# The out projection's first two column chunks computed as a pair with two quads of seven products

## The chip, the cores and the metric

One core of one Trainium2 chip runs the kernel. The metric is the device time of one execution in microseconds (us). The engines are called as in the profile: PE (TensorE), DVE (VectorE), ACT (ScalarE), POOL (GpSimd), SP (SyncE).

## The reference

A decoder layer on 256 rows of 2048 features in float32, cut here to what matters:

```python
merged = sigmoid(ga) * (o_a @ w_br_fox) + sigmoid(gb) * (o_b @ w_br_dil)   # 256 x 2048
x = x + merged @ w_out                                                     # w_out 2048 x 2048
h = rms_norm(x, g_ffn)
u = h @ w_up                                                               # and then conv, silu, w_down
```

## The kernel before

**Precision and units.** Each float32 product is made of three float32r matmuls: with a = a_h + a_l and w = w_hi + w_lo, it sums a_h w_hi, a_h w_lo and a_l w_hi. Weights are taken in *units*: a tile of 256 rows (two k steps) by 512 columns, 512 KB. For unit n SP loads the tile, ACT makes the high half (`high(n)`, L1250), DVE the low half (`low(n)`, L1764), PE uses both. The halves lie in a ring of RING = 6 units: `high(n)` waits until unit n - 6 has been used. ACT and DVE walk one fixed list; at the position of unit n stand first the bank sums that wait for unit n, then `high(n + 6)` or `low(n + 6)`, then other work. PE, SP and POOL walk lists of their own.

**A plain unit** is used for both halves of the rows (r = 0, 1): 2 x 2 x 3 = 12 matmuls of 128x512.

**A quad of seven products.** For two column chunks side by side, a 2 x 2 block of weights (rows kt and kt + 4, columns of side 0 and side 1) with a 2 x 2 block of activations takes seven products in place of eight (P1 to P7, six matmuls each and quarter q). Two quarters (QU = 2) cover k steps 0 to 7. Operands on the weight side are tiles and sums of tiles, made in place in `raw_x[q]` and `raw_y[q]`. The order is P3 (raw_y as loaded), then POOL adds the tile of the other side to raw_y by an adding transfer (`third_sum`, y_summed); P1 takes raw_x as loaded; P7 takes raw_y; then DVE adds raw_x to raw_y (behind `low` of P7, y_added), P6 takes that; POOL adds a tile to raw_x (`first_sum`, waits for y_added, x_summed), P5 takes it; raw_x is loaded anew, P2 takes it, and in the gates DVE adds raw_x to raw_y once more for P4. The rest of the k steps goes in plain units (G, side, j).

**The stages around the change.** The seven gate pairs (`GATES`) use such quads already: five are for q, k and the gates of the two mixers. Then the branch projections: 4 chunks of w_fox and 4 of w_dil with 4 units each, all plain. After each chunk c of w_dil `dil_part(c)` on DVE multiplies two banks with the gate (L2103, dil_merged) and adds both branches into `tmp` (L2107, merged); one chunk later, after unit 2, PE turns tmp with eight transposes (L796, banks 4 and 5), ACT copies the high half to actA (`merged_high`, L1276, mt_hi), DVE makes the low half (`merged_low`, L1816, mt_lo). Chunk 3 is turned within the out projection.

**The out projection** then takes chunks 0, 1 and 2 in turn, 8 plain units each, with bank pairs (6, 7), (1, 3), (0, 2). Chunk 0 waits for mt_lo 6 (chunks 0 to 2 of merged are split), chunk 1 for dil_merged 4. `add_x2` adds the banks to x, which ACT's queue loads anew (2 MB, L1561) after the second unit. x2 is turned, scaled and squared chunk by chunk. Chunk 3 lies between the first products of the up projection. SP loads the out tiles with `load_late` (L560), and the first tiles of the up projection behind them.

## Time and profile before

| | |
|---|---|
| Time, median of 3 runs | 1336.95 us (1336.2 to 1337.53) |
| The profiled execution | 1336.57 us |
| Its span | 1334.6 us |
| PE busy | 1329.1 us, 100% |
| PE weight load busy | 1101.9 us, 83% |
| DVE busy | 1122.2 us, 84% |
| ACT busy | 940.6 us, 70% |
| POOL busy | 156.2 us, 12% |
| Moved by DMA | 305.73 MB, 229 GB/s |

The span is from the first to the last record of the profile; the execution's own time has 1.97 us beside it. Matmuls are pipelined: PE's busy time overlaps, so that its pace is read from the starts of matmuls.

### The profile page before, as it was taken

Reading aid. Unit: us, or ns where it says so; the run is one execution under the profiler, and the core shown is the slowest. Engines: PE = TensorE matmul, PEld = TensorE weight load, DVE = VectorE, ACT = ScalarE, POOL = GpSimd, SP = SyncE. Lnnn points to the kernel's source line nnn. Section 1 sums busy time; section 2 is a strip of 40 time slices with the busy share of each in tenths; the row PEclk is TensorE's granted clock in tenths of the full one; section 3 lists DMA queues with packets and bytes.
Section 4 is the critical chain, followed back from the end, with each engine's and each line's share of the span. In section 5 each row is a group of like instructions: output and inputs, shape, how many; then the busy total and the mean of one; then the engine's idle time right before and its main releaser. Section 6 shows DMA issues by size and latency. Waiting matters only on the chain.

```text
span 1334.6 us, 16448 instructions
## 1 busy us (share of the span) xinstructions
PE 1329.1 (100%) x6055; PEld 1101.9 (83%) x6055; DVE 1122.2 (84%) x1333; ACT 940.6 (70%) x1180; POOL 156.2 (12%) x175
## 2 busy tenths in 40 slices
PE   9999999999999999999999999999999999999999
PEld 7888888888888888888888888888888888888887
DVE  6768787888878876657789898999999999999996
ACT  6666666666666654446777778888888888888872
POOL 0121212021011000001010101111111102020200
PEclk9999999999999999999999999999999999999999
DMA  9877685758888655567879798999999999999952
GB/s 355 285 171 261 142 257 122 246 149 231 233 214 231 210 175 172 209 227 226 270 177 332 158 306 169 312 221 283 246 254 266 229 288 215 299 210 313 199 198 101
DMA packets 118175, 305.73 MB, mean 229 GB/s; under 512 B 11848, under 2 KB 13136, under 8 KB 117584
## 3 DMA queue, kind: packets, MB, share of 16 engines
q1 hardware_dynamic: 92288, 234.57, 50.4%
q0 software_dynamic: 21728, 66.07, 27.9%
q10 hardware_dynamic: 4080, 4.05, 0.9%
q8 instruction: 48, 0.79, 0.2%
q14 instruction: 31, 0.25, 0.1%
HBM read 302.55 MB, written 2.11 MB: 228 GB/s over the span
## 4 chain that ended last, share of the span: by engine, by line
PE 98%; DMA 1%; DVE 1%; ACT 0%; issue 0%; SPq 0%; ACTq 0%
PE acc L743 14%; PE acc L747 14%; PE acc L745 13%; PE acc L783 9%; PE acc L787 9%; PE acc L785 9%; PE acc L964 4%; PE acc L968 4%; PE acc L966 4%; PE acc L939 3%; PE acc L941 3%; PE acc L943 3%; PE acc L1076 1%; PE acc L768 1%; PE acc L766 1%; PE acc L764 1%
## 5 line engine op out<-in xcount | busy, mean ns | idle before, releaser
L1764 DVE TENSOR_TENSOR w_lo<-raw,w_hi 128x1024 fp32r<-128x1024 f32 x234 | 284.0, 1221 | 89.6 <-ACT w_hi L1250 88.4
L1250 ACT ACTIVATE w_hi<-raw 128x1024 fp32r<-128x1024 f32 x234 | 244.8, 1055 | 109.5 <-PE acc L747 75.9
L743 PE MATMUL acc<-w_hi,actA 128*128 128x512 f32 x664 | 261.7, 394 | 0.4 <-DVE w_lo L1764 0.3
L747 PE MATMUL acc<-w_hi,actA 128*128 128x512 f32 x664 | 259.1, 390 | 0.0
L745 PE MATMUL acc<-w_lo,actA 128*128 128x512 f32 x664 | 258.7, 390 | 0.0
L1250 ACT ACTIVATE w_hi<-raw_y 128x1024 fp32r<-128x1024 f32 x144 | 149.6, 1058 | 74.9 <-PE acc L747 22.4
L1764 DVE TENSOR_TENSOR w_lo<-raw_y,w_hi 128x1024 fp32r<-128x1024 f32 x144 | 173.2, 1220 | 23.1 <-ACT w_hi L1250 21.7
L1764 DVE TENSOR_TENSOR w_lo<-raw_x,w_hi 128x1024 fp32r<-128x1024 f32 x108 | 130.0, 1221 | 41.1 <-ACT w_hi L1250 40.9
L743 PEld LDWEIGHTS acc<-w_hi,actA 128*128 128x128 f32 x664 | 124.8, 188 | 26.3 <-issue 1.4
L747 PEld LDWEIGHTS acc<-w_hi,actA 128*128 128x128 f32 x664 | 124.7, 188 | 26.3
L745 PEld LDWEIGHTS acc<-w_lo,actA 128*128 128x128 f32 x664 | 124.8, 188 | 25.0
L1250 ACT ACTIVATE w_hi<-raw_x 128x1024 fp32r<-128x1024 f32 x108 | 111.2, 1051 | 37.8 <-DMA raw_x<-w_in 19.1
L783 PE MATMUL acc<-w_hi,actB 128*128 128x512 f32 x296 | 116.2, 393 | 0.0
L787 PE MATMUL acc<-w_hi,actB 128*128 128x512 f32 x296 | 115.4, 390 | 0.0
L785 PE MATMUL acc<-w_lo,actB 128*128 128x512 f32 x296 | 115.3, 389 | 0.0
L964 PE MATMUL acc<-w_hi,actA 128*128 128x512 f32 x224 | 88.4, 395 | 0.0
L968 PE MATMUL acc<-w_hi,actA 128*128 128x512 f32 x224 | 87.3, 390 | 0.0
L966 PE MATMUL acc<-w_lo,actA 128*128 128x512 f32 x224 | 87.2, 389 | 0.0
L2405 POOL DMA_DIRECT2D raw_y<-w_up x34 | 29.5, 867 | 458.9 <-DVE w_lo L1764 458.6
L1250 ACT ACTIVATE w_hi<-odd 128x1024 fp32r<-128x1024 f32 x63 | 66.3, 1053 | 18.5 <-PE acc L787 9.8
L1764 DVE TENSOR_TENSOR w_lo<-odd,w_hi 128x1024 fp32r<-128x1024 f32 x63 | 76.8, 1218 | 1.8 <-ACT w_hi L1250 1.8
L2178 DVE SCALAR_TENSOR_TENSOR work<-acc,smalls_sb,work 128x255 f32<-128x255 f32 (+1 forms) x176 | 72.5, 474 | 3.4 <-ACT work L1583 3.3
(296 smaller groups left out, 2598.8 us busy)
## 6 DMA issues: line engine op xcount, KB each, us to landing
raw<-w_in SPq DMA_DIRECT2D x102, 512.0 KB, 4.8
raw<-w_down SPq DMA_DIRECT2D x59, 512.0 KB, 5.7
raw_x<-w_up SPq DMA_DIRECT2D x44, 512.0 KB, 5.0
raw_y<-w_up POOLq DMA_DIRECT2D x34, 512.0 KB, 7.3
raw_x<-w_in SPq DMA_DIRECT2D x28, 512.0 KB, 4.3
raw<-w_out SPq DMA_DIRECT2D x28, 512.0 KB, 4.5
odd<-w_up SPq DMA_DIRECT2D x27, 512.0 KB, 5.2
work<-w_up SPq DMA_DIRECT2D x24, 512.0 KB, 5.4
```

The lines of the kernel that those rows point to most:

```text
L743: nc.tensor.matmul(o, lhsT=a_h, rhs=w_hi[:, s, k, :], start=first and k == 0, stop=False, skip_group_check=onto_seed)
L745: nc.tensor.matmul(o, lhsT=a_h, rhs=w_lo[:, s, k, :], start=False, stop=False, skip_group_check=onto_seed)
L747: mm = nc.tensor.matmul(o, lhsT=a_l, rhs=w_hi[:, s, k, :], start=False, stop=last and k == KU - 1, skip_group_check=onto_seed)
L783: nc.tensor.matmul(o, lhsT=a_h, rhs=w_hi[:, s, k, :], start=first and k == 0, stop=False, skip_group_check=True)
L785: nc.tensor.matmul(o, lhsT=a_h, rhs=w_lo[:, s, k, :], start=False, stop=False, skip_group_check=True)
L787: mm = nc.tensor.matmul(o, lhsT=a_l, rhs=w_hi[:, s, k, :], start=False, stop=last and k == KU - 1, skip_group_check=True)
L964: nc.tensor.matmul(o, lhsT=a_h, rhs=w_hi[:, s, k, :], start=side == 0 and j == 0 and k == 0, stop=False, skip_group_check=True)
L966: nc.tensor.matmul(o, lhsT=a_h, rhs=w_lo[:, s, k, :], start=False, stop=False, skip_group_check=True)
L968: mm = nc.tensor.matmul(o, lhsT=a_l, rhs=w_hi[:, s, k, :], start=False, stop=kt == KT - 1, skip_group_check=True)
L1250: nc.scalar.activation(w_hi[:, n % RING, :, :], src.rearrange("p (k n) -> p k n", k=KU), ACT.Copy).then_inc(hi_done, 1)
L1764: nc.vector.tensor_tensor(w_lo[:, n % RING, :, :], src.rearrange("p (k n) -> p k n", k=KU), w_hi[:, n % RING, :, :].bitcast(f32), ALU.subt ...
L2178: t = nc.vector.scalar_tensor_tensor(out=conv[:, j, lag:SEQ], in0=bank[(4, 7)[j // 2]][:, (j % 2) * SEQ:(j % 2 + 1) * SEQ - lag], scalar=s ...
```

## The change

Chunks 0 and 1 of the out projection become pair number PAIRS = 7, with two quads (k steps 0 to 7) and four plain units on each side (k steps 8 to 15). The units' order is P3, P1, P7, P6 (two quarters each), G 0 0, P5, G 0 1, G 1 0, P2, G 0 2, P4, G 0 3, G 1 1, G 1 2, G 1 3, and then the eight units of chunk 2 (C). The names G00, G01, G10 below are plain units by side and j.

- Activations: `merged_high` for merged chunks 0 and 1 copies each bank twice, once to `odd` in float32; after chunk 1 `make_merged` forms four sums, each from the last; four `merged_part_high` on ACT and four `merged_part_low` on DVE split them, and ACT copies -P1 (two copies).
- P3 waits for the four parts (h_part_lo 8) in place of mt_lo 6, P1 for dil_merged 4.
- P1's sum is copied by ACT from bank 0 to bank 1 and P6's from bank 0 to bank 3; the next product in bank 0 and the plain units wait for the copies (g_p1, g_v).
- P4's operand is summed by an adding transfer of POOL to raw_y behind the low half of P6 (y_summed), where the gates have an addition on DVE.
- The load of x is issued after P3's second quarter.
- Counts of the semaphores that the up projection shares with the pair (y_added, x_summed and so on) go up accordingly, and the first raw_x and raw_y tiles of the up projection are loaded behind P2 and P4 of the pair.

The diff, cut to its core:

```diff
 BR_UNIT = GATE_UNIT + len(GATES)
 OUT_UNIT = BR_UNIT + 4 * UPR
-FF_UNIT = OUT_UNIT + 3 * UPR
+
+
+def out_units():
+
+    def product(name):
+        return [("H", PAIRS, name, q) for q in range(QU)]
+
+    def plain(side, *js):
+        return [("G", PAIRS, side, j) for j in js]
+
+    units = product("P3") + product("P1") + product("P7") + product("P6") + plain(0, 0)
+    units += product("P5") + plain(0, 1) + plain(1, 0) + product("P2") + plain(0, 2)
+    units += product("P4") + plain(0, 3) + plain(1, 1, 2, 3)
+    return units + [("C", u) for u in range(UPR)]
+
+
...
+OUTS = out_units()
+OUT_LOADS = [unit for unit in OUTS if unit[0] != "H"]
+OUT_LOAD_AT = {unit: k for k, unit in enumerate(OUT_LOADS)}
+OUT_AT = {unit: OUT_UNIT + n for n, unit in enumerate(OUTS)}
+FF_UNIT = OUT_UNIT + len(OUTS)
...
                     load_gate_b22(c + 1, q)
             for m in range(RAW_SLOTS, 4 * UPR):
                 load_late(BR_UNIT + m, br_tile(m))
...
+
+            def load_out(k):
+                unit = OUT_LOADS[k]
+                if unit[0] == "G":
+                    _, c, side, j = unit
+                    src = pair_tile(side, c, 2 * QU + j)
+                else:
+                    src = pair_tile(2, PAIRS, unit[1])
+                s = raw_use(OUT_AT[unit])[0]
+                sp.dma_start(raw[:, s, :].rearrange("p (k n) -> p k n", k=KU), src).then_inc(w_loaded[s], 16)
+
+            for k in range(RAW_SLOTS):
+                sp.wait_ge(lo_done, OUT_UNIT - RAW_SLOTS + k)
+                load_out(k)
+            for n, unit in enumerate(OUTS, OUT_UNIT):
+                if unit[0] != "H":
+                    k = OUT_LOAD_AT[unit] + RAW_SLOTS
+                    if k < len(OUT_LOADS):
+                        sp.wait_ge(lo_done, n)
+                        load_out(k)
+                    continue
+                _, c, name, q = unit
+                if name == "P5":
+                    sp.wait_ge(lo_done, n)
+                    load_gate_b21(c, q)
+                elif name == "P2":
+                    sp.wait_ge(lo_done, n)
+                    load_b11(0, q)
+                elif name == "P4":
+                    sp.wait_ge(lo_done, n)
+                    load_b22(0, q)
             sp.wait_ge(o_lo, NHEADS)
             for k in range(2):
                 load_unit(LOADS[k])
...
+            def out_product(n, name, q):
+
+                if q == 0:
+                    if name == "P3":
+                        pe.wait_ge(o_lo, NHEADS)
+                        pe.wait_ge(h_part_lo, 8)
+                    elif name == "P1":
+                        pe.wait_ge(dil_merged, 4)
+                        pe.wait_ge(h_part_hi, 12)
+                    elif name == "P7":
+                        pe.wait_ge(g_c22, PAIRS)
+                    elif name == "P6":
+                        pe.wait_ge(g_p1, PAIRS + 1)
+                    elif name == "P5":
+                        pe.wait_ge(g_v, PAIRS + 1)
+                o = bank[OUT_BANKS[name]]
+                pe.wait_ge(lo_done, n)
...
+            def out_plain(n, side, j):
+
+                pe.wait_ge(mt_lo, 6 if j < 2 else 8)
+                pe.wait_ge(lo_done, n)
+                s = n % RING
+                for r, o in enumerate((bank[6], bank[0]) if side else (bank[1], bank[3])):
+                    if r and j == 0:
+                        pe.wait_ge(g_u0 if side else g_v, PAIRS + 1)
...
+            for n, unit in enumerate(OUTS, OUT_UNIT):
+                if unit[0] == "H":
+                    out_product(n, unit[2], unit[3])
+                    if unit == ("H", PAIRS, "P1", QU - 1):
                         pe.wait_ge(merged, 4)
                         transpose_block(lambda r, col: tmp[:, r, col:col + P], bank[4:6], mt_ready)
-                    elif u == 2:
-                        turn_x2(c - 1)
+                elif unit[0] == "G":
+                    out_plain(n, unit[2], unit[3])
...
+                    if unit == ("G", PAIRS, 1, PLAIN - 1):
+                        turn_x2(0)
+                else:
+                    u = unit[1]
+                    if u == 0:
+                        pe.wait_ge(g_c22, PAIRS + 1)
+                    rows_unit(n, actA, (KU * u, KU * u + 1), (bank[2], bank[0]), u == 0, u == UPR - 1)
+                    if u == 2:
+                        turn_x2(1)
 
             def turn_up(rows, ready):
 
...
                     kt = 4 * c + 2 * b
+                    if c < 2:
+                        nc.scalar.activation(merged_turned(c)[:, 2 * b:2 * b + 2, :],
+                                             bank[4 + b][:, :].rearrange("p (j s) -> p j s", j=2), ACT.Copy)
                     nc.scalar.activation(actA[:, kt:kt + 2, 0:SEQ],
                                          bank[4 + b][:, :].rearrange("p (j s) -> p j s", j=2),
                                          ACT.Copy).then_inc(mt_hi, 1)
+
+            def merged_part_high(name, made):
+                act.wait_ge(h_made, made)
+                nc.scalar.activation(merged_part(name)[:, :, 0:P], merged_sum[name], ACT.Copy).then_inc(h_part_hi, 1)
 
             def x2_squares(c):
...
-            for c in range(3):
-                for u in range(UPR):
-                    high(OUT_UNIT + UPR * c + u + RING)
-                    if u == 1 and c == 0:
-                        act.wait_ge(merged, 4)
-                        act.dma_start(xr[:, :, :], x_rows).then_inc(x_again, 16)
-                    if u == 2 and c == 0:
-                        merged_high(3)
-                    elif u == 2:
-                        x2t_copy(c - 1, bank[4:6])
-                    elif u == 4 and c == 2:
-                        part_high("P3")
-                        part_high("P1")
-                    elif u == 5 and c == 2:
-                        part_high("P7")
-                        part_high("P6")
-                x2_squares(c)
+                    elif c == 3 and u == 0:
+                        merged_part_high("P5", 9)
+                        merged_part_high("P7", 10)
+                        merged_part_high("P6", 11)
+                        merged_part_high("P3", 12)
+                    elif c == 3 and u == 1:
+                        act.wait_ge(mt_lo, 2)
+                        for half in range(2):
+                            nc.scalar.activation(own[:, 0, :, half * P:half * P + P],
+                                                 gate_quarter(0, 0, half).bitcast(f32), ACT.Copy, scale=-1.0)\
+                                .then_inc(h_part_hi, 1)
+
+            def out_sum(n, name):
+
+                act.wait_ge(used, n + 1)
+                if name == "P1":
+                    act.wait_ge(dil_merged, 3)
+                    nc.scalar.activation(bank[1], bank[0], ACT.Copy, scale=-1.0).then_inc(g_p1, 1)
+                else:
+                    nc.scalar.activation(bank[3], bank[0], ACT.Copy, scale=-1.0).then_inc(g_v, 1)
+
+            for n, unit in enumerate(OUTS, OUT_UNIT):
+                if unit in (("H", PAIRS, "P1", QU - 1), ("H", PAIRS, "P6", QU - 1)):
+                    out_sum(n, unit[2])
+                high(n + RING)
+                if unit == ("H", PAIRS, "P3", QU - 1):
+                    act.wait_ge(merged, 4)
+                    act.dma_start(xr[:, :, :], x_rows).then_inc(x_again, 16)
+                elif unit == ("H", PAIRS, "P1", QU - 1):
+                    merged_high(3)
+                elif unit == ("G", PAIRS, 1, 2):
+                    x2_squares(0)
+                elif unit == ("G", PAIRS, 1, PLAIN - 1):
+                    x2t_copy(0, bank[4:6])
+                elif unit == ("C", 1):
+                    x2_squares(1)
...
+            def make_merged():
+
+                x11, x21, x12, x22 = (merged_sum[name] for name in ("P6", "P7", "P3", "P5"))
+                nc.vector.tensor_tensor(x22, x21, x22, ALU.subtract).then_inc(h_made, 1)
+                dve.wait_ge(h_made, 9)
+                nc.vector.tensor_tensor(x21, x11, x21, ALU.subtract).then_inc(h_made, 1)
+                dve.wait_ge(h_made, 10)
+                nc.vector.tensor_tensor(x11, x11, x22, ALU.subtract).then_inc(h_made, 1)
+                dve.wait_ge(h_made, 11)
+                nc.vector.tensor_tensor(x12, x12, x11, ALU.subtract).then_inc(h_made, 1)
+
+            def merged_part_low(name, n_hi):
+                dve.wait_ge(h_part_hi, n_hi)
+                to = merged_part(name)
+                nc.vector.tensor_tensor(to[:, :, P:2 * P], merged_sum[name], to[:, :, 0:P].bitcast(f32), ALU.subtract)\
+                    .then_inc(h_part_lo, 1)
+
             for c in range(4):
                 for u in range(4):
                     if u == 3:
                         if c:
                             merged_low(c - 1)
                             dve.wait_ge(mt_ready, 2 * c)
+                        if c == 2:
+                            make_merged()
                         dil_part(c)
                     low(BR_UNIT + 16 + 4 * c + u + RING)
                     if c == 0 and u == 0:
                         out_low(15)
+                    elif c == 3 and u == 1:
+                        merged_part_low("P5", 7)
+                        merged_part_low("P7", 8)
+                        merged_part_low("P6", 9)
+                        merged_part_low("P3", 10)
 
             def add_x2(n, c, banks):
                 dve.wait_ge(used, n + 1)
...
+            def out_rows(r, side):
+                return xr[:, r, side * NB:side * NB + NB]
+
+            def add_bank(b, rows):
+                return nc.vector.tensor_tensor(rows, bank[b], rows, ALU.add)
+
+            def out_bank_sums(n, unit):
+
+                if unit == ("H", PAIRS, "P5", QU - 1):
+                    dve.wait_ge(x_again, 16)
+                    dve.wait_ge(used, n + 1)
+                    add_bank(0, out_rows(0, 1)).then_inc(g_u0, 1)
+                elif unit == ("G", PAIRS, 0, 1):
+                    nc.vector.tensor_tensor(out_rows(1, 1), out_rows(1, 1), bank[7], ALU.subtract).then_inc(g_u1, 1)
+                elif unit == ("G", PAIRS, 1, 0):
+                    add_bank(7, out_rows(1, 0)).then_inc(g_v7, 1)
+                elif unit == ("G", PAIRS, 0, PLAIN - 1):
+                    dve.wait_ge(used, n + 1)
+                    add_bank(1, out_rows(0, 0))
+                    dve.wait_ge(g_v7, PAIRS + 1)
+                    add_bank(3, out_rows(1, 0)).then_inc(x2_done, 1)
+                elif unit == ("G", PAIRS, 1, PLAIN - 1):
+                    dve.wait_ge(used, n + 1)
+                    dve.wait_ge(g_u1, PAIRS + 1)
+                    add_bank(0, out_rows(1, 1)).then_inc(g_c22, 1)
+                    dve.wait_ge(g_u0, PAIRS + 1)
+                    add_bank(6, out_rows(0, 1)).then_inc(x2_done, 1)
+                elif unit == ("C", UPR - 1):
+                    add_x2(n, 2, (bank[2], bank[0]))
+
+            for n, unit in enumerate(OUTS, OUT_UNIT):
+                out_bank_sums(n, unit)
+                low(n + RING)
+                if unit == ("H", PAIRS, "P7", 0):
+                    merged_low(3)
+                elif unit == ("C", 3):
+                    make_sums()
+                elif unit == ("C", 5):
+                    part_low("P3")
+                    part_low("P1")
+                elif unit == ("C", 6):
+                    part_low("P7")
+                    part_low("P6")
 
             def x2_norm():
 
...
                 prepare_dil(12 + c).then_inc(prep_ready, 1)
+            third_sum(PAIRS, 0)
+            third_sum(PAIRS, 1)
+            first_sum(PAIRS, 0)
+            first_sum(PAIRS, 1)
+            for q in range(QU):
+                pool.wait_ge(lo_done, OUT_AT["H", PAIRS, "P6", q])
+                nc.gpsimd.dma_start(raw_y[:, q, :].rearrange("p (k n) -> p k n", k=KU),
+                                    w_out_v[:, KU * (QU + q):KU * (QU + q) + KU, 0:NB], accum_op=ALU.add)\
+                    .then_inc(y_summed[q], 16)
 
             def add_tile(side, i, kt_pair, to, done):
```

## Rows read from the trace of the kernel before

**Rows 1.** Page: the chain that ended last, shares by engine.
```profile
PE 98%; DMA 1%; DVE 1%; ACT 0%; issue 0%; SPq 0%; ACTq 0%
```

**Rows 2.** Windows (stretch, length, PE, PEld, DVE, ACT, POOL busy, clock, DMA share, GB/s).
```profile
293.20:334.00 40.80, 40.80 (x184) 33.85 (x182) 32.29 (x29) 26.69 (x32) 4.83 (x4) 1.00 0.75 205
...
553.60:598.90 45.30, 45.27 (x208) 37.66 (x209) 24.37 (x23) 20.73 (x26) 0.00 (x0) 1.00 0.65 229
```

**Rows 3.** Timeline of PE, 549.5 to 555.5 (start, length, what).
```profile
549.76 1.03 PE L796 MATMUL acc<-smalls_sb,tmp 128*128 128x128 f32 x8
550.55 0.48 PE L743 MATMUL acc<-w_hi,actB 128*128 128x512 f32 x1
...
552.69 0.39 PE L743 MATMUL acc<-w_hi,actB 128*128 128x512 f32 x1
...
553.14 0.39 PE L747 MATMUL acc<-w_hi,actB 128*128 128x512 f32 x1
553.63 0.47 PE L743 MATMUL acc<-w_hi,actA 128*128 128x512 f32 x1
```

**Rows 4.** Timeline of PE, 0 to 14: the nine warm-up matmuls.
```profile
1.32 4.21 PE L864 MATMUL acc<-actB 128*128 128x512 f32 x9 [1.32 <-POOL actB L2354]
```

**Rows 5.** Timeline of DVE before the out projection, chunk 2 of the branch.
```profile
539.30 1.23 DVE L1764 TENSOR_TENSOR w_lo<-raw,w_hi 128x1024 fp32r<-128x1024 f32 x1 [1.50 <-ACT w_hi L1250]
540.45 1.28 DVE L1816 TENSOR_TENSOR actA<-acc,actA 128x512 fp32r<-128x512 f32 x2
541.86 1.29 DVE L2103 TENSOR_TENSOR work<-acc,work 128x512 f32<-128x512 f32 x2
...
544.33 1.22 DVE L1764 TENSOR_TENSOR w_lo<-raw,w_hi 128x1024 fp32r<-128x1024 f32 x1
...
553.63 1.29 DVE L2103 TENSOR_TENSOR work<-acc,work 128x512 f32<-128x512 f32 x2
```

**Rows 6.** Timeline of DVE, 613 to 621: sums and parts of x2.
```profile
613.40 0.68 DVE L1892 TENSOR_TENSOR odd<-work 128x512 f32<-128x512 f32 x1
614.12 0.69 DVE L1894 TENSOR_TENSOR odd<-work,odd 128x512 f32<-128x512 f32 x1
...
620.05 0.68 DVE L1832 SCALAR_TENSOR_TENSOR actB<-work,actB 128x512 fp32r<-128x512 f32 x1
620.65 1.22 DVE L1764 TENSOR_TENSOR w_lo<-raw_x,w_hi 128x1024 fp32r<-128x1024 f32 x1
```

**Rows 7.** Timeline of DVE, gate pair: P7's low half and its addition.
```profile
340.50 1.23 DVE L1764 TENSOR_TENSOR w_lo<-raw_y,w_hi 128x1024 fp32r<-128x1024 f32 x1 [0.20 <-ACT w_hi L1250]
341.76 1.23 DVE L1773 TENSOR_TENSOR raw_y<-raw_y,raw_x 128x1024 f32<-128x1024 f32 x1
342.90 2.44 DVE L1764 TENSOR_TENSOR w_lo<-raw_y,w_hi 128x1024 fp32r<-128x1024 f32 x2
```

**Rows 8.** Timeline of ACT, branch stage: two halves of a turned chunk.
```profile
539.18 1.06 ACT L1276 ACTIVATE actA<-acc 128x512 fp32r<-128x512 f32 x2
```

**Rows 9.** Timeline of ACT, gate pair: two high halves in succession.
```profile
339.40 2.01 ACT L1250 ACTIVATE w_hi<-raw_y 128x1024 fp32r<-128x1024 f32 x2 [2.40 <-DMA raw_y<-w_in]
```

**Rows 10.** DMA: issue of x; adding transfers (L2366); issues 558 to 563.
```profile
559.48 0.39 ACTq L1561 DMA_DIRECT2D work<-x  x1
...
DMA to landing us min/median/max: 5.8/6.2/9.5
...
work<-x ACTq DMA_DIRECT2D x1, 2048.0 KB, 10.7
raw<-w_out SPq DMA_DIRECT2D x1, 512.0 KB, 10.7
...
raw<-w_out SPq DMA_DIRECT2D x1, 512.0 KB, 9.7
```

**Rows 11.** Groups of ACT by line and form: copy from bank to bank.
```profile
L1616 ACT ACTIVATE acc<-acc 128x512 f32<-128x512 f32 x11 | 6.6, 602 | 0.0
```

132 lines of the change are left out of this document (74 added, 58 removed).

## The prediction

> **What bounds the kernel now.** I read the page first: a span of 1334.6 us and a chain of work that is 98% PE [rows 1]. Then the windows: in the stretch of the first two chunks of the out projection, and in a whole pair of gate columns, PE is busy practically all the time at a granted clock of 1.00 [rows 2]. Then PE's timeline: two matmuls start 0.45 us apart with one between them, so one starts every 0.227 us; a unit of twelve takes 2.72 us, eight transposes 0.79 us. The only hole near the change is the start of the out projection: the last branch matmul starts at 553.14, the first one of the out projection at 553.63 instead of 553.37 (it waits for the low part of the third merged chunk, mt_lo 6): 0.26 us [rows 3]. So the span is the number of matmuls plus PE's waits. A matmul saved is worth 0.227 us, and every wait put before PE costs its whole length. DVE and ACT are read for one question only: are they in time when PE asks? All times below are on the clock of the profile of before, with P3 able to start at 553.37.
>
> **Removed from PE.** Two plain chunks are 16 units x 12 = 192 matmuls. The pair is 14 product units x 6 + 8 plain units x 12 = 180. Saved: 12 x 0.227 = 2.72 us. The 0.26 us hole goes too, since P3 no longer waits for mt_lo 6. Gain: 2.98 us. The two sets of transposes stay.
>
> **Added to DVE before the pair.** This is the term to work through, since DVE runs its list in order. Columns: what it does, when it starts.
> At 539.30 the low half of P3 first quarter is made [rows 5]. ACT now makes four copies of a turned chunk instead of two; two took 1.06 [rows 8], so the last comes at about 541.3, and DVE's second merged_low of this chunk starts at 541.35 and takes 0.6. Then make_merged: four 128x512 subtractions, each waiting for the last; a dependent one starts 0.72 after its forerunner, an independent one 0.60 [rows 6], so 3 x 0.72 + 0.6 = 2.8: 541.95 to 544.75. Before, DVE began dil_part(2) at 541.86; now 544.75. It takes 2.47 (541.86 to 544.33, where the next low half starts [rows 5]): to 547.2. Three low halves (P3 second, P1 both) start 1.14 apart [rows 7]: to 550.65 (ACT has the high halves ready: that of P1's first quarter at 544.6, four merged_part_high at the pace of such copies, two in 1.06 [rows 8], to 547.75, the next high half to 548.85). Four merged_part_low at 0.6: to 553.05. **P3 asks at 553.37: hidden, with 0.3 us to spare.** Next the low half of P7 first quarter with the addition behind it; a low half, its addition and the step to the next instruction take 2.40 [rows 7]: 555.5, and this is y_added for quarter 0. Then merged_low(2), two at 0.6: 556.7. Only now dil_part(3), which DVE did at 553.63 before [rows 5]: two products of 1.29 together: **dil_merged reaches 4 at 558.05**. None of this waits for anything; DVE is simply full from 541.3 on.
>
> **P1's wait.** P1 starts bank 0, which the last branch chunk fills, so it waits for dil_merged 4. PE asks after P3's twelve matmuls, at 556.1. New wait 558.15 - 556.1 = 2.05 us. Queued behind on PE is everything. P1 then runs to 560.85, the transposes to 561.65 (merged 4 comes at 559.3), P7 to 564.4.
>
> **P6's wait.** On DVE follow the sum tmp (to 559.2), P7's second low half and its addition: y_added of quarter 1 at 561.65. On ACT the high half of P6's second quarter waits for that addition; behind it in ACT's list stand the issue of the x load, the high half of the first plain unit and only then the copy of P1's sum from bank 0 to bank 1, which P6 waits for. 561.7 + 2 x 0.96 (high halves start 0.96 apart [rows 9]) + 0.4 for the issue of the x load [rows 10] and 0.1 for the steps between = 564.2, + 0.60 for a bank to bank copy [rows 11] = 564.8. PE asks at 564.4: 0.5 us with the restart.
>
> **The wait that decides.** Row 1 of the first plain unit waits for g_v, the copy of P6's sum to bank 3. In ACT's list that copy stands behind the high halves of P5's second quarter, G01 and G10. P5's high half needs raw_x of that quarter after the adding transfer, which POOL can issue only at y_added = 561.7. From issue to landing such a transfer took 5.8 to 9.5 us, median 6.2 [rows 10]. But here 2 MB of x are asked for at about 562.7, 1 us behind it. A plain tile issued 0.4 us before the x load in the profile took 10.7 us, as long as the x load itself, and the next one, issued 2.3 us behind x, 9.7 us [rows 10]. A transfer under x is the nearest row, so I take 10: landing 571.7. Then three high halves, 3 x 0.96, and the copy, 0.6, with the steps between 0.1: g_v at 575.3. PE would be there (P6 564.9 to 567.7, row 0 to 569.0) at 569.0: **6.3 us**. Bounds: with 5.8 the landing is 567.5, g_v 571.1, the wait 2.1; with 13 (x's 10.7 lengthened by the two adding transfers for P4 and the tiles that are now under way with it) the wait is 9.3.
>
> The Trainium skill, DMA: Bandwidth & Descriptors, "Issuing engines are not separate DMA queues", says that transfers of all issuing engines run on the same 16 DMA engines and interleave; the rows above agree (10.7 us beside x), and if they did not interleave, the sum would go by the 5.8 bound.
>
> **Behind it.** The second quarter's P2 load waits in SP's queue for P5's low half (about 574), landing 578.5; high halves and low halves to 582, then the bank sum g_u0 at 582.7, which the row 1 of G10 asks for at 583.7: hidden by 1 us. The P4 operand by transfer is asked for at 563 and 564 and used after 580: hidden, also from its own price; against the gate pair it spares DVE two additions of 1.22, which lie beside PE and buy nothing here. At chunk 2 PE waits for g_c22: DVE starts 0.27 after the last matmul and takes 0.65, the transposes of x2 cover 0.79: 0.2 us. What ACT, SP and POOL have more of in the branch stage is covered: PE's units there last 2.72 with 1.06 of ACT, and DMA is at 0.65 in the stretch of the change [rows 2]. The copy of -P1 to its own tile ends at 550. From chunk 2 on nothing changes but the place of x2_squares(1), on ACT, beside 2.72 us units.
>
> **Sum.** -2.98 + 2.05 + 0.5 + 6.3 + 0.2 = +6.1 us. The profiled execution took 1336.57 (span 1334.6 and 1.97 around it), the median of the three runs is 1336.95: 1342.7 on the first, **1343.0** on the median. 0.2% is 2.7 us, about what this kernel's measurement can tell from no change.
>
> **Rivals.**
> *A, faster: the cover holds.* In the gate pair the same products run with the same rings without a hole in PE: 40.8 us of 40.80 busy [rows 2]. If DVE reaches dil_part(3) by 554.7 instead of 556.7, P1 does not wait, y_added of quarter 1 comes at 559.6, the adding transfer, issued 3 us ahead of x, lands in 5.8 at 565.4, and g_v is there at 569.0. Then nothing waits but chunk 2's start: -2.98 + 0.2 = -2.8, 1334.2. For it: the gates' pairs, with the same pace of loads and halves. Against: there no chunk is merged, turned and split on DVE in the six units ahead, and no x is loaded. 2 us less on DVE's list of 15.4 us (541.3 to 556.7) is the point from which it decides.
> *B, no change: the backlog comes, but the adding transfer lands early (5.8).* The wait on g_v is 2.1: +1.9, 1338.9. If DVE is 1 us faster besides, it is near 0.
> *C, slower still: the clock falls.* The nine warm-up matmuls, which ran after idleness, took 4.21 us [rows 4] where nine at 0.227 take 2.04. If a wait of 6.3 us on g_v leaves PE at the 1.2 GHz level for as long, another 2.2 us: +8.3, 1345.2. PE's waits near the change are 0.26 us and none [rows 2, 3], so this profile is silent on what a long one does. The Trainium skill, TensorE: Matmul & The Clock Gate, Part 1, says that the clock is halved after an idle stretch and comes back with sustained work; the warm-up row agrees, and by that rule this rival and not the main case would come.
> *D: the change doesn't do what it says.* All products and loads are in the list PE walks; twelve fewer matmuls are certain. Not given a chance.
>
> **Chances.** The DVE sum rests on a list without gaps, each duration from a row; the landing under x is the loose term. Main case 0.43, C 0.25, B 0.16, A 0.16. Slower by over 0.2% is main and C with a little of B: 0.70; within 0.2%: 0.15; faster: 0.15. Range: the low bound of B less 1 us of DVE error, about 1337, to C with the long landing, 1336.95 + 9.1 + 2.2 = 1348: 1337 to 1348. The main case alone: 1339.5 to 1346.
>
> **What the new profile would show.** DVE's timeline without a gap from the second merged_low of the chunk to dil_part(3), whose products start near 556.7 instead of 553.6 after a P3 at 553.4; an idle of PE before P1 released by DVE's gb products, of about 2 us; one of 2 to 9 us in the first plain unit's second row, released by ACT's copy of bank 0 to bank 3, with ACT itself waiting for DMA raw_x before three high halves; the x load under way at the same time. Right on the gain: 12 matmuls fewer. The granted clock in the stretch behind that wait tells C. Wrong if ACT does not wait for raw_x, if DVE shows idle time between 545 and 556, or if PE's wait before P1 is absent.

## The result: 1346.57 us, 9.9 us slower, with the wait where it was forecast and the slow clock behind it

The changed kernel takes 1346.57 us (median of six runs, 1346.28 to 1348.75), the kernel before beside it 1336.72 (six runs, 1336.2 to 1337.53): a ratio of 1.0077, 95% interval 1.0066 to 1.0088. Forecast were 1343.0 and a range of 1337 to 1348. The profiled execution took 1347.68 with a span of 1345.7.

The page of the kernel after: the span, the DMA queues (packets, MB, share of 16 engines), and the chain that ended last.

```profile
span 1345.7 us, 16482 instructions
...
q1 hardware_dynamic: 91744, 233.53, 49.9%
q0 software_dynamic: 23360, 69.21, 29.0%
...
PE 95%; DVE 2%; DMA 2%; ACT 1%; issue 1%; SPq 0%; ACTq 0%; DVEq 0%
```

PE's share of the chain fell from 98% [rows 1] to 95%. What PE waited for, by line and releaser (us in total, times, the longest):

```profile
PE acc L1162 <- ACT acc L1700: 8.5, 1, 8.5
PE acc L1142 <- DVE work L2257: 1.6, 1, 1.6
PE acc L931 <- POOL actB L2558: 1.3, 1, 1.3
PE acc L810 <- issue: 0.6, 1, 0.6
```

The first two are new and lie in the changed stage: row 1 of G00 waits for ACT's copy of P6's sum, and P1 waits for DVE's products of the last branch chunk. The third is in the unchanged start, and the fourth, at 457.41, lies ahead of the change too. PE's timeline of the kernel after puts a place to each:

```profile
550.65 1.03 PE L863 MATMUL acc<-smalls_sb,tmp 128*128 128x128 f32 x8
...
554.26 0.39 PE L1142 MATMUL acc<-w_hi,actB 128*128 128x512 f32 x1
...
556.75 0.39 PE L1146 MATMUL acc<-w_hi,actB 128*128 128x512 f32 x1
558.73 0.50 PE L1142 MATMUL acc<-w_hi,own_parts 128*128 128x512 f32 x1 [1.59 <-DVE work L2257]
...
565.04 0.39 PE L1146 MATMUL acc<-w_hi,own_parts 128*128 128x512 f32 x1
565.27 0.39 PE L1142 MATMUL acc<-w_hi,actB 128*128 128x512 f32 x1
...
569.12 0.39 PE L1166 MATMUL acc<-w_hi,actA 128*128 128x512 f32 x1
...
578.04 0.79 PE L1162 MATMUL acc<-w_hi,actA 128*128 128x512 f32 x1 [8.53 <-ACT acc L1700]
578.63 0.63 PE L1164 MATMUL acc<-w_lo,actA 128*128 128x512 f32 x1
579.06 0.63 PE L1166 MATMUL acc<-w_hi,actA 128*128 128x512 f32 x1
...
582.90 0.45 PE L1146 MATMUL acc<-w_hi,actB 128*128 128x512 f32 x1
583.18 0.39 PE L1142 MATMUL acc<-w_hi,actB 128*128 128x512 f32 x1
```

How to read it against the forecast. The branch's last transposes start at 550.65, where they started at 549.76 before [rows 3]: 0.89 us came in ahead of the change and belong to this execution (in the profiles of runs 2 and 7 below, with the same code up to there, they start at 549.86 and 549.87), so every time of the prediction is to be read 0.9 later here. P3 follows the last branch matmul at the usual step: no hole. P1 would start at 556.98 and starts at 558.73: 1.75. P6 starts at 565.27 without a wait. Row 1 of G00 would start at 569.35 and starts at 578.04: 8.69. Behind it matmuls start 0.43 apart, and from 583.18 on 0.23 apart again.

Windows of the kernel after (stretch, length, busy time of PE, PEld, DVE, ACT, POOL, granted clock, DMA share, GB/s):

```profile
557.00:569.00 12.00, 10.41 (x50) 8.55 (x50) 9.98 (x10) 5.14 (x7) 4.81 (x4) 1.00 0.71 195
569.00:578.00 9.00, 0.51 (x3) 0.09 (x1) 2.35 (x4) 3.43 (x4) 0.00 (x0) 0.71 1.07 259
578.00:583.00 5.00, 4.96 (x12) 3.89 (x13) 3.56 (x4) 1.28 (x2) 0.00 (x0) 0.50 1.09 306
583.00:590.00 7.00, 7.00 (x32) 5.77 (x31) 6.05 (x7) 3.91 (x4) 0.00 (x0) 1.00 0.89 313
```

The granted clock is 0.50, the 1.2 GHz level, for the 5 us behind the long wait. The DMA share is 1.07 and 1.09 while PE waits and behind it; in the stretch of the change it was 0.65 before [rows 2].

DVE's timeline of the kernel after shows the full list that was forecast:

```profile
541.34 1.50 DVE L1970 TENSOR_TENSOR actA<-acc,actA 128x512 fp32r<-128x512 f32 x2
542.75 0.68 DVE L2281 TENSOR_TENSOR odd<-odd 128x512 f32<-128x512 f32 x1
...
545.53 1.28 DVE L2257 TENSOR_TENSOR work<-acc,work 128x512 f32<-128x512 f32 x2
...
557.40 1.28 DVE L2257 TENSOR_TENSOR work<-acc,work 128x512 f32<-128x512 f32 x2
...
561.10 1.22 DVE L1927 TENSOR_TENSOR raw_y<-raw_y,raw_x 128x1024 f32<-128x1024 f32 x1
```

And ACT's, with the wait for the adding transfer ahead of three high halves (L1369) and the copy (L1700):

```profile
562.37 0.39 ACTq L1708 DMA_DIRECT2D work<-x  x1
...
574.56 1.06 ACT L1369 ACTIVATE w_hi<-raw_x 128x1024 fp32r<-128x1024 f32 x1 [7.76 <-DMA raw_x<-w_out]
575.52 1.99 ACT L1369 ACTIVATE w_hi<-raw 128x1024 fp32r<-128x1024 f32 x2
577.41 0.57 ACT L1700 ACTIVATE acc<-acc 128x512 f32<-128x512 f32 x1
```

DMA issues of the kernel after from 562 to 575 (KB each, median us to landing):

```profile
work<-x ACTq DMA_DIRECT2D x1, 2048.0 KB, 9.7
raw_y<-w_out POOLq DMA_DIRECT2D x2, 512.0 KB, 15.7
raw_x<-w_out POOLq DMA_DIRECT2D x1, 512.0 KB, 11.9
```

The third row is P5's adding transfer of the second quarter, issued 0.3 us behind x; the second row is P4's two.

**The books.** From the branch's last transposes to the first matmul of the up projection PE needed 72.03 us before (549.76 to 621.79) and 82.17 after (550.65 to 632.82): +10.14. That is -2.72 (twelve matmuls) - 0.26 (the hole) + 1.75 (P1) + 8.69 (g_v) + 2.42 (twelve matmuls took from 578.04 to 583.18, 5.14, for 2.72) + 0.15 (chunk 2, which starts at 609.99, 0.94 after its transposes, for 0.79) = +10.03; the missing 0.1 is of the size of what the first matmuls behind a wait take longer (P1's twelve took 2.90, not 2.72). This length, below called the stage, is free of what varies ahead of it, and is given for every experiment. Each stage is read from one profiled execution, so that small differences in it are not to be leaned on.

### The profile page after: what moved, and what is told of

It is laid out like the page before. It is cut to its first block, busy times and chain, and to the rows that moved or that the text cites. A ratio compares the mean times of both kernels' runs of the same rounds, so it can differ in the third digit from the quotient of the medians.

```text
span 1345.7 us, 16482 instructions
## 1 busy us (share of the span) xinstructions
PE 1330.0 (99%) x6043; PEld 1100.7 (82%) x6043; DVE 1137.9 (85%) x1352; ACT 952.0 (71%) x1198; POOL 163.7 (12%) x181
## 3 DMA queue, kind: packets, MB, share of 16 engines
q1 hardware_dynamic: 91744, 233.53, 49.9%
q0 software_dynamic: 23360, 69.21, 29.0%
## 4 chain that ended last, share of the span: by engine, by line
PE 95%; DVE 2%; DMA 2%; ACT 1%; issue 1%; SPq 0%; ACTq 0%; DVEq 0%
PE acc L810 12%; PE acc L814 12%; PE acc L812 12%; PE acc L850 9%; PE acc L854 9%; PE acc L852 9%; PE acc L1031 4%; PE acc L1035 4%; PE acc L1033 4%; PE acc L1010 3%; PE acc L1008 3%; PE acc L1006 3%; PE acc L1193 1%; PE acc L831 1%; PE acc L835 1%; PE acc L833 1%
## 5 line engine op out<-in xcount | busy, mean ns | idle before, releaser
L1918 DVE TENSOR_TENSOR w_lo<-raw,w_hi 128x1024 fp32r<-128x1024 f32 x226 | 273.7, 1219 | 73.5 <-ACT w_hi L1369 72.4
L1369 ACT ACTIVATE w_hi<-raw 128x1024 fp32r<-128x1024 f32 x226 | 236.0, 1054 | 86.0 <-PE acc L814 44.8
L810 PE MATMUL acc<-w_hi,actA 128*128 128x512 f32 x600 | 236.4, 394 | 0.0
L814 PE MATMUL acc<-w_hi,actA 128*128 128x512 f32 x600 | 233.9, 390 | 0.0
L812 PE MATMUL acc<-w_lo,actA 128*128 128x512 f32 x600 | 233.5, 389 | 0.0
L1369 ACT ACTIVATE w_hi<-raw_y 128x1024 fp32r<-128x1024 f32 x152 | 158.2, 1058 | 84.1 <-PE acc L814 23.1
L1918 DVE TENSOR_TENSOR w_lo<-raw_y,w_hi 128x1024 fp32r<-128x1024 f32 x152 | 182.8, 1219 | 25.0 <-ACT w_hi L1369 23.6
L1918 DVE TENSOR_TENSOR w_lo<-raw_x,w_hi 128x1024 fp32r<-128x1024 f32 x114 | 137.2, 1220 | 50.9 <-ACT w_hi L1369 50.6
L1369 ACT ACTIVATE w_hi<-raw_x 128x1024 fp32r<-128x1024 f32 x114 | 117.5, 1051 | 52.2 <-DMA raw_x<-w_in 21.3
L814 PEld LDWEIGHTS acc<-w_hi,actA 128*128 128x128 f32 x600 | 112.6, 188 | 23.9
L810 PEld LDWEIGHTS acc<-w_hi,actA 128*128 128x128 f32 x600 | 112.7, 188 | 23.2 <-issue 0.6
L812 PEld LDWEIGHTS acc<-w_lo,actA 128*128 128x128 f32 x600 | 112.8, 188 | 22.6
L1031 PE MATMUL acc<-w_hi,actA 128*128 128x512 f32 x224 | 88.5, 395 | 0.0
L1035 PE MATMUL acc<-w_hi,actA 128*128 128x512 f32 x224 | 87.3, 390 | 0.0
L1033 PE MATMUL acc<-w_lo,actA 128*128 128x512 f32 x224 | 87.2, 389 | 0.0
L1369 ACT ACTIVATE w_hi<-odd 128x1024 fp32r<-128x1024 f32 x63 | 66.3, 1053 | 20.1 <-PE acc L854 9.8
```

The source lines that it names most:

```text
L810: nc.tensor.matmul(o, lhsT=a_h, rhs=w_hi[:, s, k, :], start=first and k == 0, stop=False, skip_group_check=onto_seed)
L812: nc.tensor.matmul(o, lhsT=a_h, rhs=w_lo[:, s, k, :], start=False, stop=False, skip_group_check=onto_seed)
L814: mm = nc.tensor.matmul(o, lhsT=a_l, rhs=w_hi[:, s, k, :], start=False, stop=last and k == KU - 1, skip_group_check=onto_seed)
L1031: nc.tensor.matmul(o, lhsT=a_h, rhs=w_hi[:, s, k, :], start=side == 0 and j == 0 and k == 0, stop=False, skip_group_check=True)
L1033: nc.tensor.matmul(o, lhsT=a_h, rhs=w_lo[:, s, k, :], start=False, stop=False, skip_group_check=True)
L1035: mm = nc.tensor.matmul(o, lhsT=a_l, rhs=w_hi[:, s, k, :], start=False, stop=kt == KT - 1, skip_group_check=True)
```

## The experiments

The theory: two lists in fixed order (DVE's before P1, ACT's before g_v) and one late landing make the waits, and the half clock adds 2.4. Rivals: the adding transfers are slow by themselves; the waits stand one behind the other, so that removing one uncovers the next.

**1. x asked for later**

```diff
-                if unit == ("H", PAIRS, "P3", QU - 1):
+                elif unit == ("H", PAIRS, "P6", QU - 1):
                     act.wait_ge(merged, 4)
                     act.dma_start(xr[:, :, :], x_rows).then_inc(x_again, 16)
```

> One edit to the changed kernel: ACT issues the 2 MB load of x behind the bank copy and the high half at the position of P6's second quarter, not behind P3's second quarter. In the changed kernel the adding transfer to raw_x (second quarter) took 11.9 us with x beside it; the other three took 6.0 to 6.2. Theory (x beside it is what makes it late): it lands about 6.2 us after its issue near 562.6, so near 569; the copy g_v comes near 572.5, the wait of PE on it shrinks from 8.7 us to about 3, the granted clock stays at 1.00 or falls only briefly, and x lands near 584, before or within 2 us of the bank sum that needs it. Time about 1338 to 1341. Rival (the adding transfers for P4 queued right behind it, or the SP tiles, are what slow it): the landing stays above 9 us, the wait above 6 us, the time above 1344.

1350.4 us, ratio 1.0102 (1.0087 to 1.0117), stage 85.03. PE's timeline:

```profile
572.07 0.50 PE L1162 MATMUL acc<-w_hi,actA 128*128 128x512 f32 x1 [2.73 <-ACT acc L1700]
...
589.46 0.80 PE L1162 MATMUL acc<-w_hi,actA 128*128 128x512 f32 x1 [7.29 <-DVE work L2324]
```

DMA issues of this run from 555 to 575:

```profile
raw_x<-w_out POOLq DMA_DIRECT2D x2, 512.0 KB, 6.0
raw_y<-w_out POOLq DMA_DIRECT2D x2, 512.0 KB, 10.3
```

The landing was as the theory has it: P5's adding transfer of the second quarter took 6.1 us (11.9 with x beside), and the wait on g_v fell from 8.5 to 2.7. So the adding transfers are not slow by themselves; P4's two are still right behind it here. But x, issued at 576.76, was now what the bank sum g_u0 lacked, and row 1 of G10 waited 7.3 us. The clock fell behind the wait of 2.7 too. The time is a miss (1338 to 1341 expected): I had not followed x to the instruction that reads it.

**2. The copy ahead of the three high halves**

```diff
-                high(n + RING)
+                if unit == ("H", PAIRS, "P6", QU - 1):
+                    for late in (3, 2, 1):
+                        high(n - late + RING)
+                if unit not in (("H", PAIRS, "P7", 0), ("H", PAIRS, "P7", 1), ("H", PAIRS, "P6", 0)):
+                    high(n + RING)
```

> One edit to the changed kernel: in ACT's list the copy of P6's sum to bank 3 (g_v) stands ahead of the high halves of P5 second quarter, G01 and G10, which follow it in their order; nothing else moves. Theory (the copy itself had all it needed at 568 and only stood behind ACT's wait for raw_x): the wait before the second row of G00 goes; PE then runs G00 and P5's first quarter and waits for the low half of P5's second quarter, which comes 2.4 us after the landing near 574.5, so about 5 us instead of 8.7. Time 1341 to 1344. Rival (the copy waits for something else, such as a bank or PE): the wait stays at 8 to 9 us and the time at 1346 to 1347.

1346.62 us, 1.0073 (1.0058 to 1.0088), stage 82.03. The wait on g_v is gone, and PE's timeline has two others:

```profile
575.90 0.80 PE L1142 MATMUL acc<-w_hi,actB 128*128 128x512 f32 x1 [4.49 <-DVE w_lo L1922]
...
585.96 0.50 PE L1162 MATMUL acc<-w_hi,actA 128*128 128x512 f32 x1 [2.19 <-DVE work L2328]
```

The first is P5's second quarter, which needs the same late transfer itself; the second is the bank sum. The place in ACT's list was a cause of the wait on g_v and not of the loss. The wait before P5 was forecast at about 5, the one on the bank sum was not, and the time of 1341 to 1344 was a miss.

**3. The last chunk's products earlier in DVE's list**

```diff
-                        if c:
+                        if 0 < c < 3:
                             merged_low(c - 1)
...
+                    if c == 3 and u == 3:
+                        dve.wait_ge(mt_ready, 6)
+                        merged_low(2)
```

> One edit to the changed kernel: DVE makes the low halves of merged chunk 2 (merged_low(2)) behind dil_part(3) and the low half and addition of P7's second quarter, not ahead of dil_part(3); PE waits for them before the next transposes. Theory (P1 waits for DVE's full list, and y_added of the second quarter comes at the end of that list): the two copies of 0.6 us leave the list ahead of both, so P1's wait shrinks from 1.75 to about 0.55 us, while the transfer is issued 1.2 us earlier and x not earlier than the same addition. The wait on g_v changes by at most 1.2 us. Time 1344 to 1346. Rival (P1 waits for PE's own last branch unit or for ACT): the wait before P1 stays at 1.7 us.

1345.75 us, 1.0066 (1.0051 to 1.0081), stage 80.74. P1's wait went from 1.6 to 0.4 and the one on g_v from 8.5 to 5.8; the transposes behind P1 now waited 1.9 for the merged_low that was moved. As expected (1344 to 1346): the wait before P1 is DVE's list. In the whole time the gain is within the spread (1344.24 to 1346.87).

**4. Matmuls in place of the wait**

```diff
+                    if r and j == 0 and not side:
+                        for _ in range(34):
+                            nc.tensor.matmul(bank[2][:, :], lhsT=own_parts[:, 0:P], rhs=own_parts[:, 0:NB],
+                                             start=True, stop=True)
```

> One edit to the changed kernel: 34 more matmuls of 128x512 into a bank that nothing uses yet, between the two rows of G00, ahead of the wait on g_v; their results are overwritten, and the output stays the reference's. They fill 34 x 0.227 = 7.7 us of the wait of 8.7 us. Theory (the half clock behind the wait is a cost of its own, 12 matmuls at 0.43 in place of 0.227): the wait shrinks to 1 us, g_v does not move, the clock stays at 1.00 and the time falls by about 2.4 us to 1344. Rival (the clock behind the wait is not the wait's doing, or PE was held back there by something else): the matmuls behind g_v still start 0.43 us apart and the time stays at 1346.5 or rises.

1347.68 us (1345.75 to 1347.76), 1.0081 (1.0064 to 1.0098), stage 81.10 in the profiled run. Windows of the same stretches as above:

```profile
569.00:578.00 9.00, 7.76 (x34) 6.12 (x34) 2.71 (x4) 3.44 (x4) 0.00 (x0) 1.00 1.07 261
578.00:583.00 5.00, 5.00 (x23) 4.13 (x22) 3.21 (x3) 1.46 (x2) 0.00 (x0) 1.00 1.08 329
```

The clock stays at 1.00 and 23 matmuls fit where 12 did, so the idleness is what let it fall. The stage is only 1.07 shorter, not 2.4: row 1 started 0.37 later in it (the landing took 12.3 us), and G10's row 1 then waited 0.6 for the bank sum, which it had not waited for while the clock was slow. In the whole time no gain can be seen, and the forecast of 1344 was a miss.

**5. DVE's new sums and parts on GpSimd**

```diff
-                nc.vector.tensor_tensor(x22, x21, x22, ALU.subtract).then_inc(h_made, 1)
+                nc.gpsimd.tensor_tensor(x22, x21, x22, ALU.subtract).then_inc(h_made, 1)
...
-                nc.vector.tensor_tensor(to[:, :, P:2 * P], merged_sum[name], to[:, :, 0:P].bitcast(f32), ALU.subtract)\
+                nc.gpsimd.tensor_tensor(to[:, :, P:2 * P], merged_sum[name], to[:, :, 0:P].bitcast(f32), ALU.subtract)\
```

> One edit to the changed kernel: POOL, not DVE, makes the four sums of make_merged and the four low halves of the parts (POOL stands idle there). Theory (DVE's full list makes P1 wait and y_added of the second quarter late): DVE's list before dil_part(3) is 5.2 us shorter, dil_part(3) starts as soon as PE's last branch unit is done, the wait before P1 goes to 0, and y_added of quarter 1 comes at about 560 instead of 562.3 (PE's last branch unit, two products, the sum, a low half and its addition still stand before it). With x issued right behind, the transfer still takes 10 to 12 us: the wait on g_v stays at 7 to 9 us, since PE arrives 1.75 us earlier as well. Time 1344 to 1346. Rival (the late transfer is only the backlog's doing): the wait on g_v falls under 5 us and the time under 1342.

1352.0 us, 1.0112 (1.0095 to 1.0129), stage 85.95. Timelines of POOL and of DVE:

```profile
547.86 2.17 POOL L2589 TENSOR_TENSOR odd<-odd 128x512 f32<-128x512 f32 x1
...
556.48 1.73 POOL L2598 TENSOR_TENSOR own_parts<-odd,own_parts 128x512 fp32r<-128x512 f32 x1
557.74 2.90 POOL L2598 TENSOR_TENSOR actB<-odd,actB 128x512 fp32r<-128x512 f32 x2
```

```profile
548.80 2.32 DVE L1918 TENSOR_TENSOR w_lo<-raw_y,w_hi 128x1024 fp32r<-128x1024 f32 x1
...
556.13 5.59 DVE L1918 TENSOR_TENSOR w_lo<-raw_x,w_hi 128x1024 fp32r<-128x1024 f32 x1 [2.79 <-ACT w_hi L1369]
```

A miss. Low halves that take 1.22 alone took 2.32 and 5.59. The first ends 1.1 after POOL's subtraction beside it (550.03), the second 1.1 after POOL's last (560.64): they did not share, DVE's instruction stood until POOL's were done. The Trainium skill, SBUF — State Buffer, "SBUF: two separate sides", says that of a VectorE instruction with two SBUF inputs and a GpSimd instruction that reads SBUF the one that starts first holds their common port for its whole length, and the other is blocked. These rows agree with the blocking; in the second case POOL's subtractions that started later, from 556.48 on, went ahead of DVE's of 556.13 all the same. P3 waited 2.8, P1 2.9, and row 1 of G00 5.7 on g_v.

**6. x in two halves, the first behind P7's first quarter, the second behind G01** (an issue moved and split; VectorE waits for the second half at chunk 2)

> One edit to the changed kernel: x is loaded in two halves by columns, the first (chunks 0 and 1, 1 MB) behind the high half that waits for the late adding transfer, the second behind G01. Theory (x beside the transfer costs 5.7 us, and moving all of x behind it only moved the wait to the bank sum, 7.3 us in e1): the transfer lands in 6.2 us, the wait on g_v is 2.7 us as in e1, the first half of x lands in about 6 us, near 576, and the bank sum waits at most 1 us; P1's 1.7 us stays. Half clock behind g_v costs up to 2 us. Time 1338 to 1341. Rival (what made it late is the number of transfers, whatever their size): over 1344.

1346.05 us, 1.0072 (1.0056 to 1.0087), stage 81.30: 2.6 on g_v, then 3.9 on the bank sum, since P2's plain loads landed late (ACT waited 8.8 us for one, to 580.13). The adding transfer took 5.9 with nothing of x beside it, but the half of x issued behind it took 12.0. A miss (1338 to 1341 expected): half as much x in this stretch is not enough less.

**7. 2, 5 and the split together**

> Three edits to the changed kernel together: the sums and low halves on POOL (as e5), x in two halves behind the late transfer (as e6, the first half issued right behind P5 second quarter's high half), and the copy g_v ahead of those three high halves (as e2). Theory (the waits found are all that stands between the 12 saved matmuls and the time): no wait of PE over 0.3 us in the pair, clock at 1.00; time = before - 2.7 - 0.26 + 0.2, that is about 2.8 us below before, 1334. Rival (the pair's own demand on DMA, or contention that no edit here touches, is a further cost): another wait of over 1 us appears and the time stays above that of before.

1351.47 us, 1.0111 (1.0096 to 1.0126), stage 86.50. No wait on g_v, but 2.8 before P3 and 1.3 before P1 (the blocking of run 5), and 8.5 on the bank sum. A miss (1334 expected): the waits found so far were not all that stood between the saved matmuls and the time.

**8. P4's operand by VectorE**

```diff
-            for q in range(QU):
-                pool.wait_ge(lo_done, OUT_AT["H", PAIRS, "P6", q])
-                nc.gpsimd.dma_start(raw_y[:, q, :].rearrange("p (k n) -> p k n", k=KU),
-                                    w_out_v[:, KU * (QU + q):KU * (QU + q) + KU, 0:NB], accum_op=ALU.add)\
-                    .then_inc(y_summed[q], 16)
```

> One edit to the changed kernel: P4's operand is summed by DVE behind P2's low half, as in the gate pairs, and the two adding transfers behind P6 are left out. Theory (they are issued behind the late transfer of raw_x and land long before P4): the wait on g_v shrinks by at most 1 us, since less is under way beside x and the transfer; DVE's two additions of 1.22 us delay the low half of G02 and the bank sum g_u0 behind it by up to 2.4 us, which adds a wait of 0 to 2 us before G10's second row. Time 1345 to 1348, no clear change. Rival (the two transfers, each worth more than one plain load, are what doubles the landing time): the landing falls to 8 us, the wait on g_v to 5, the time to 1343.

1346.74 us, 1.0078 (1.0063 to 1.0093), as expected the time of the changed kernel; stage 80.97. The wait on g_v is 8.0, and P5's transfer still took 11.4 us. In runs 2, 3 and 4 and in the changed kernel, where P4's two transfers are behind it, it took 11.2 to 12.3; in runs 1, 6, 7 and 9, with P4's two but no x beside it, 5.9 to 6.2. So x nearly doubles the landing, and P4's two add nothing that can be told. The profiled stage is 1.2 shorter, 0.5 of it on g_v and most of the rest behind it, where the slow clock lasted 3.2 us and not 4.9; the medians show no such gain. In the whole time P4's operand by transfer neither gains nor costs here, and the two additions that it spares DVE are hidden too.

**9. The half of x that the pair reads, issued in the branch stage** (at 535.98 instead of 562.37; the other half behind G03)

```diff
+                    if c == 2 and u == 1:
+                        act.wait_ge(merged, 2)
+                        act.dma_start(xr[:, :, 0:2 * NB], x_rows[:, :, 0:2 * NB]).then_inc(x_again, 16)
```

> One edit to the changed kernel: x for chunks 0 and 1 (1 MB) is loaded in the branch stage, as soon as the gate columns under it are used up (merged 2), where DMA is half idle, and the rest of x at G03. Nothing of x is under way from 555 to 590. Theory (2 MB of x in the stretch where the pair's transfers are most dense is the loss; e1 and e6 only moved it onto the P2 loads and the bank sum): the adding transfer lands in 6.2 us, the wait on g_v is 2.7 us, the P2 loads land in 6 to 8 us, no wait on g_u0; P1's 1.7 us stays; half clock behind g_v costs 1.5 to 2.4 us. Time 1336.7 - 3.0 + 1.7 + 2.7 + 2.0 + 0.2 = 1340.3, 1339 to 1342. Rival (the pair's own transfers fill DMA by themselves): a wait of over 2 us is left on P5, P2 or G10, time over 1343.

1342.68 us (1340.19 to 1345.08), 1.0044 (1.003 to 1.0058), stage 78.70: 3.9 us less than the changed kernel. The wait on g_v is 2.8; 1.6 stay before P1, 1.6 on the bank sum, and 1.3 are new before chunk 2. Windows:

```profile
554.00:562.00 8.00, 6.41 (x33) 5.05 (x32) 7.89 (x10) 2.07 (x3) 1.20 (x1) 1.00 0.48 77
562.00:570.00 8.00, 7.05 (x32) 5.49 (x30) 5.15 (x5) 5.99 (x8) 3.66 (x3) 1.00 0.79 138
570.00:580.00 10.00, 8.13 (x30) 6.61 (x31) 5.39 (x6) 3.73 (x5) 0.00 (x0) 0.83 1.07 312
```

Without x, DMA is full from 570 on all the same, from the pair's own transfers and the tiles that SP lets go when low halves are done. The time lies between the two forecasts (1339 to 1342, and over 1343 if the pair's own transfers fill DMA).

**10. 9 with both lists reordered** (DVE: last chunk's products one low half and its addition earlier; ACT: both copies of sums ahead of the high halves that they stood behind)

> e9 and three moves in the lists: DVE does dil_part(3) ahead of P7 first quarter's low half and addition; ACT copies P1's sum ahead of P6 second quarter's high half; ACT copies P6's sum (g_v) ahead of the high halves of P5 second quarter, G01 and G10. Nothing is left out or put on another engine. Theory (list order is the rest of the loss): no wait before P1, none on g_v, up to 1 us before P5's second quarter (its transfer is issued at 562.3, lands at 568.5, its low half is ready at 571, PE asks at 570), clock at 1.00. Time 1336.7 - 3.0 + 0.2 + 0 to 1 = 1334 to 1335. Rival (a cost of the pair that no edit here touches): the time stays at or above that of before although PE shows no wait over 1 us.

1344.93 us, 1.0059 (1.0046 to 1.0072), stage 79.21. P1's wait is gone, g_v's 1.3, but the bank sum's 4.8: P2's load landed at 577.5, after ACT had waited 5.5 us for it. Two things are in this. PE was at the bank sum's place 3.5 us earlier than in run 9. And the edit itself made the load late: with the last chunk's products ahead of P7's first addition, POOL could issue P5's first transfer only at 560.25 (556.53 in run 9), and SP the load of P2 behind it only at 568.74 (566.70).

```profile
560.25 1.20 POOL L2583 DMA_DIRECT2D raw_x<-w_out  x1 [9.89 <-DVE raw_y L1936]
```

So the bank sum ran at 582.19, 0.3 earlier than in run 9, for a PE that was there 3.5 earlier. A miss by 10 us.

**11. 10 with P4's operand by VectorE**

> e10 with P4's operand summed by DVE as in the gate pairs, and without the two adding transfers behind P6. Theory (once nothing is late, P4's operand has more than 10 us by either way): the same time as e10 within 0.5 us. If the transfer for P4 is worth something, DVE's two additions of 1.22 us delay the low halves of P2 second quarter and G02 and the bank sum g_u0: up to 1.5 us slower. If instead the adding transfers cost DMA time that the P2 loads lack, it is faster by up to 1 us.

1342.78 us (1342.14 to 1343.23), 1.0044 (1.0031 to 1.0058), stage 76.86: 2.15 us less than run 10. The windows of run 10 and then of run 11:

```profile
570.00:580.00 10.00, 7.67 (x33) 5.74 (x31) 6.01 (x7) 4.19 (x6) 0.00 (x0) 1.00 1.07 318
```

```profile
570.00:580.00 10.00, 7.09 (x31) 5.26 (x29) 9.93 (x10) 6.36 (x7) 0.00 (x0) 1.00 0.76 257
```

P2's loads were there at 572.55 and 575.14 and the bank sum's wait went from 4.8 to 3.2, now from DVE's list with the two additions back in it. The executions of the two runs do not overlap (run 10 from 1343.83 up), and the gain is more than either forecast had (the same within 0.5, or up to 1 faster). With x out of this stretch and DMA full, the two adding transfers cost more than the additions that they spare.

**12. 11 with the bank sum one place earlier**

```diff
-                if unit == ("H", PAIRS, "P5", QU - 1):
+                if unit == ("G", PAIRS, 0, 0):
                     dve.wait_ge(x_again, 16)
-                    dve.wait_ge(used, n + 1)
+                    dve.wait_ge(used, OUT_AT["H", PAIRS, "P5", QU - 1] + 1)
```

> Edit: the kernel of e11 (half of x loaded in the branch stage, the two lists of VectorE and ScalarE reordered, the fourth product's operand by VectorE), and VectorE's sum of the half used bank (g_u0), which row 1 of unit G10 waits for, stands one low half earlier in VectorE's list, ahead of the low half of P2's second quarter instead of behind it, its addition and the low half of G02. List theory: in e11 P5's last matmul was done by about 575.5 and the sum started at 580.23; it now starts near 576.6 and G10's second row near 577.6 instead of 580.97; the wait of 3.2 us goes to 0.3, and PE's half clock behind it (about 2 us) goes too if a shorter wait doesn't bring it; the low half of P2's second quarter comes at 578.5, still before PE asks for it. So 3 us less than e11's 1342.8 if the clock falls all the same, 5 less if it doesn't: 1338 to 1340, and even so not below the kernel before, since a wait of 1 us on g_v, the steps of 0.6 and 0.7 and the later start of the out projection are left. Rival (the matter is DMA): the next late thing is a low half whose tile has not landed, the wait moves to P2's first product, and the time stays within 1 us of e11's.

1342.36 us (1338.45 to 1342.98), 1.0036 (1.0023 to 1.0048), stage 76.63. Expected were 1338 to 1340, a miss. The wait of 3.2 is gone and the low half of P2 came in time. PE's timeline has another in its place, and DVE's shows why:

```profile
602.28 0.78 PE L811 MATMUL acc<-w_hi,actA 128*128 128x512 f32 x1 [2.87 <-DVE work L2334]
602.86 0.63 PE L813 MATMUL acc<-w_lo,actA 128*128 128x512 f32 x1
```

```profile
600.40 1.23 DVE L1925 TENSOR_TENSOR w_lo<-raw,w_hi 128x1024 fp32r<-128x1024 f32 x1 [1.26 <-ACT w_hi L1368]
601.54 1.28 DVE L2334 TENSOR_TENSOR work<-acc,work 128x512 f32<-128x512 f32 x2
```

Chunk 2 waits for the last bank sums (g_c22). PE's last matmul of the pair started at 598.14, but the sums stand in DVE's list behind a low half whose tile landed only at 599.3, so they started at 601.54, and the clock fell behind that wait too. The gain of 0.4 on run 11 is within the spread: the rival's pattern, a landing that is late elsewhere, though not at P2, where I had put it.

## Why the prediction was right

**The direction and the place: right.** The kernel became slower, 9.9 us where 6.1 were forecast. Named were three waits and their releasers, and the two longer ones came; the long one is released by the copy of line 1700, with ACT waiting for raw_x ahead of it, x under way beside. Run 1 (no x beside, landing 6.1) and run 2 (copy first, no wait there) show both of its parts.

**The gain: right.** -2.72 and -0.26, read off directly.

**P1's wait, 2.05: measured 1.75.** The list on DVE was forecast to reach the last products at 556.7; less 0.9 it did at 556.5. Run 3 shows it is the list. Rival A (DVE quick enough, 1334.2) fell with that: 0.2 of its 2 us was there. Its sum was wrong besides: without the waits before P1 and P6, PE would be at row 1 at 569.0 - 2.55 = 566.45 and not at 569.0, so that with g_v at 569.0 a wait of about 2.6 stays, and the rival comes to about no change (-0.2).

**P6's wait, 0.5: absent.** This wait is a step that failed, by little. Two terms were too large: y_added came at 562.3, less 0.9 561.4 and not 561.7; and the 0.4 for issuing x took no time from ACT, whose high half starts at 562.36 and x's issue at 562.37, side by side.

**The wait that decides, 6.3: measured 8.7.** The term that was mis-sized is the landing: 10 us taken, 11.9 measured, 1.9 of the 2.4. The other 0.5 is P6's wait: as it was absent, PE came 0.5 earlier and waited here for as long. The 10 us were taken from plain tiles beside x [rows 10]; an adding transfer took longer, in a stretch where DMA shares of 1.07 and 1.09 moved only 259 and 306 GB/s (before: 229 at 0.65 [rows 2]). That share of 0.65 was read as room for what the change adds; it was not. My bound of 13 had x lengthened by P4's two transfers and the tiles: x took 9.7 and not longer, and without P4's two the landing was still 11.4 (run 8).

**Rival C came with the main case: 2.2 forecast for the clock, 2.42 measured.** The main case alone, 1343.0 and 1339.5 to 1346, did not come: 1346.57 lies above it, and the range reached 1348 only because it took in C (9.1 us by the long landing alone is 1346.05). I held C at 0.25 because the profile of before shows no long wait. Run 4 shows it by the clock row, 1.00 for 0.50, with matmuls in place of the wait. The rule of the Trainium skill, TensorE: Matmul & The Clock Gate, Part 1, that idleness halves the clock, would have given 1345.2; the rows agree with it, and it deserved the larger chance. Rival B (landing in 5.8) is what run 1 made, and even that did not lead to 1338.9.

**What was called hidden.** P4 by transfer: hidden, 0 in the changed kernel (run 8), but 2.15 us of cost once x was out of the stretch (run 11 against 10). The bank sum g_u0: no wait in the changed kernel. But "hidden by 1 us" held only as long as PE was late itself: in seven of the runs that cut the wait on g_v (1, 2, 6, 7, 9, 10 and 11) it was a wait of 1.6 to 8.5 us. Chunk 2: 0.2 forecast, 0.15 measured.

**What stays open.** No version came below the kernel before. The shortest stage, 76.63, is 4.6 above its 72.03, and 7.4 above the 69.2 that the matmuls alone would give (72.03 - 2.98 + 0.15). Whether an order of loads (SP's among them) exists that keeps DMA clear for each tile in turn was not tried. Of the 0.89 us ahead of the change, 0.6 is a wait at 457.41, which runs 3 and 5 have with 1.1 and 2.1 us; what makes it is not shown. The profiled starts of the last transposes vary from 549.86 to 554.18 (run 5) over the experiments, and the lowest is 0.1 from the kernel before, so it isn't taken as part of the change's price.

## What to carry to other kernels

Follow a moved load to the instruction that reads it, and ask what stands behind the late instruction in its engine's list: the longest wait was on one copy that was ready to run and stood behind three instructions that weren't, but the price was the late landing itself, and moving the copy alone gave nothing, because the product behind it needed the same landing. Price a transfer that shares the DMA engines by bytes under way in that stretch, adding ones dearer, not by its own median. When matmuls set the time, twelve saved (2.7 us) are gone with a single wait of 3 us, and the slow clock behind it took 1.1 to 2.5 us more in these runs.

## What was not expected of the hardware

- **GpSimd's adding transfers are dear.** On the page of after, q0 (GpSimd's queue, which carries them) moved 69.21 MB in 29.0% of the engines' time and q1 233.53 MB in 49.9%: 0.42% against 0.21% for each MB, about twice. All 132 transfers that GpSimd issues in this kernel are adding ones, so it stays open whether the adding or GpSimd's queue makes them dear. In landing: 6.1 us for 512 KB without x (run 1), 11.4 beside 2 MB of x (run 8), 11.9 beside x with P4's two behind, 15.7 for those.
- **The half clock came behind short waits too.** Matmuls started 0.43 apart behind waits of 2.2 (run 2, from 1.3 us after the restart), 2.7 (run 1), 2.9 (run 12) and 3.2 (run 11), as behind the 8.5, and 0.23 apart behind those of 1.9 (run 3) and 1.6. The length of the wait alone does not decide: behind the 2.8 before P3 in run 5 eleven steps were 0.23, behind the 2.8 before P3 in run 7 they were 0.43 from 0.8 us on; and behind waits of 8.0 (run 8) and 8.5 the slow clock lasted 3.2 and 4.9 us.
- **VectorE and GpSimd not side by side.** Subtractions of two SBUF operands ran one after the other (run 5): GpSimd's 128x512 took 1.26 from start to start while VectorE's stood, and up to 2.17 where it stood itself; VectorE's 1.22 became 2.32 and 5.59.
